# Second half of an expert gather: whole 8 KB rows instead of two 4 KB halves, and a new deal of the picks

## The reference

```python
qh = (t @ w_q).reshape(T, PEER_HEADS, 2, PEER_KEY_DIM // 2)
s = jnp.einsum('thpd,hpnd->thpn', qh, sub_keys)
s_top, i_top = lax.top_k(s, PEER_TOPK)                         # 16 of 128 keys, twice
cand = s_top[:, :, 0, :, None] + s_top[:, :, 1, None, :]
best, pos = lax.top_k(cand.reshape(T, PEER_HEADS, 256), PEER_TOPK)
idx = ...                                                      # 8 heads x 16 = 128 experts a token
g = jax.nn.softmax(best, axis=-1)
ue = jnp.take(u_tab, idx, axis=0)                              # rows of 1024 floats
ve = jnp.take(v_tab, idx, axis=0)
act = jax.nn.gelu(jnp.einsum('thkd,td->thk', ue, t))
out = jnp.einsum('thk,thkd->td', g * act, ve)
```

## Time and profile before

| | us |
|---|---|
| median of 3 runs | 3298.09 |
| lowest, highest | 3291.09, 3308.55 |
| the profiled execution | 3280.68 |
| its span | 3278.9 |
| PE busy | 2841.7 (87%) |
| DVE busy | 2060.0 (63%) |
| ACT busy | 1282.5 (39%) |
| gathers' queue, share of the DMA engines | 41.7% |
| granted TensorE clock, mean | 0.93 of full speed |

### The profile page before, as it was taken

The page is one execution under the profiler, slowest core; times in us unless marked ns, Lnnn a source line. Parts: engine busy times, 40 slices in busy tenths (PEclk is TensorE's granted clock), DMA queues, the critical chain, the costliest instruction groups (busy, mean ns, idle before and its releaser), DMA issues. The chain is left out here.

```text
span 3278.9 us, 41066 instructions
## 1 busy us (share of the span) xinstructions
PE 2841.7 (87%) x13812; PEld 2036.1 (62%) x13812; DVE 2060.0 (63%) x4500; ACT 1282.5 (39%) x2910; POOL 856.8 (26%) x773
## 2 busy tenths in 40 slices
PE   6999898887888887788899999787888997799998
PEld 6777777532344442455565666455777896678886
DVE  6785454478686775777644444754666878664445
ACT  3346423343334343546444222353544443442222
POOL 0000000243434345546656566651000000000000
PEclk9999799998999999889998999898898998799999
DMA  6531022699999999879989999985313453132221
GB/s 242 203 110 64 33 90 78 242 397 410 391 405 418 420 398 410 301 301 371 364 320 386 359 409 409 379 295 185 110 57 98 160 185 119 65 103 90 96 96 52
DMA packets 181883, 788.61 MB, mean 241 GB/s; under 512 B 19392, under 2 KB 22592, under 8 KB 148672
## 3 DMA queue, kind: packets, MB, share of 16 engines
q0 software_dynamic: 110592, 536.92, 41.7%
q1 hardware_dynamic: 65424, 229.90, 20.0%
q10 hardware_dynamic: 5680, 19.40, 1.7%
HBM read 784.05 MB, written 2.10 MB: 240 GB/s over the span
## 5 line engine op out<-in xcount | busy, mean ns | idle before, releaser
L2180 DVE SCALAR_TENSOR_TENSOR slots<-slots,work 128x1024 f32<-128x1024 f32 x508 | 621.9, 1224 | 202.5 <-DMA slots<-in_experts,consts 164.9
L895 PE MATMUL psum<-slots,acc 128*128 128x512 f32 x1008 | 492.4, 639 | 121.6 <-ACT acc L1487 115.1
L571 POOL DMA_INDIRECT slots<-in_experts,consts x252 | 286.2, 1136 | 987.2 <-DVE consts L2152 583.0
L895 PEld LDWEIGHTS psum<-slots,acc 128*128 128x128 f32 x1008 | 197.2, 202 | 398.1 <-issue 216.1
L1801 DVE TENSOR_TENSOR wlo<-w,whi 128x1024 fp32r<-128x1024 f32 x261 | 316.9, 1219 | 91.3 <-ACT whi L1283 90.5
L590 POOL DMA_INDIRECT slots<-in_expert_u,consts x256 | 286.7, 1120 | 286.5 <-DVE slots L2180 193.0
L1283 ACT ACTIVATE whi<-w 128x1024 fp32r<-128x1024 f32 x261 | 274.4, 1052 | 219.1 <-PE psum L641 212.0
L639 PE MATMUL psum<-xhi,whi 128*128 128x512 f32 x632 | 256.6, 406 | 1.9 <-DVE wlo L1801 1.9
L640 PE MATMUL psum<-xlo,whi 128*128 128x512 f32 x632 | 251.5, 398 | 0.0
L641 PE MATMUL psum<-xhi,wlo 128*128 128x512 f32 x632 | 251.4, 398 | 0.0
L626 PE MATMUL psum<-xres,w 128*128 128x256 f32 x1040 | 241.9, 387 | 0.0
(11 more groups left out here) (340 smaller groups left out, 5557.6 us busy)
## 6 DMA issues: line engine op xcount, KB each, us to landing
w<-in_stream SPq DMA_DIRECT2D x408, 512.0 KB
arena<-in_wmod SPq DMA_DIRECT2D x4, 2048.0 KB, 17.8
arena<-in_wmod ACTq DMA_DIRECT2D x8, 1024.0 KB, 6.7
acc<-in_wmod ACTq DMA_DIRECT2D x8, 1024.0 KB, 7.9
slots<-in_expert_u,consts POOLq DMA_INDIRECT x256, 8.7
slots<-in_experts,consts POOLq DMA_INDIRECT x252, 10.9
slots<-in_expert_v,consts POOLq DMA_INDIRECT x160, 9.0
xres<-in_xT SPq DMA_DIRECT2D x1, 2048.0 KB, 14.9
```

Source lines behind the costliest of these rows:

```text
L571: pool.indirect_dma_start(out=slots[slot], out_offset=None, in_=a["experts"], in_offset=bass.IndirectOffsetOnAxis(ap=indices[:, p:p + 1], ...
L895: mm = pe.matmul(bank(6 + half), diag(p), v[:, half * T:(half + 1) * T], start=(c == 0), stop=(c == PICKS - 1))
L2180: dve.scalar_tensor_tensor(u, u, 1.0, tokens[:, p // PICKS, :], ALU.mult, ALU.mult, accum_out=inner[:, c:c + 1]).then_inc(sem("dotted"), 1)
```

## The change

Three things change.

1. **Gather.** `gather_u` and `gather_v` are gone. All 512 picks use `gather`: one 8 KB row for each token into a slot, which is free when PE has used the pick. At pick 256 slot 7 is taken out of use (its place is `y_h` of the second block), which leaves eight; at pick 300 slot 9 joins, in the arena, once all 16 units are found. PE's own wait for v rows goes, since the row has landed before its dot.
2. **Deal.** The tiles' lengths are now 1.7 in lstm0, 2.4 in core0, 1.2 in lout0, 1.6 in xq0, 1.2 in xo0, 0.95 in mlp0, 2.0 in pool0, 1.7 in xq1 and 1.2 in xo1; the gap after mlp0 has 8 instead of 6.
3. **Search.** `LATE_UNITS` is 14 and units 1 to 13 stand at every 18th pick from 2 to 218; units 14 and 15 stand at 257 and 268. None stands at 279 or 290 any more.

What the planner's table gives, as the pick that the stage's last tile ends with, and the pairs that PE sums in each stage (the first tiles of a stage are multiplied together, and two picks of a gap follow them, so they count to the next stage):

| stage | tiles | picks end, before | after | pairs, before | after |
|---|---|---|---|---|---|
| lstm0 | 82-98 | 292 | 304 | 13 | 19 |
| core0 | 99-106 | 322 | 329 | 15 | 12.5 |
| lout0 (gap to 340, 347) | 107-114 | 335 | 342 | 8 | 8 |
| xq0 | 115-122 | 352 | 364 | 7 | 9.5 |
| xo0 (gap to 370, 381) | 123-130 | 365 | 376 | 8 | 7.5 |
| mlp0 | 131-194 | 469 | 461 | 50.5 | 41 |
| gap, pool0 (to 487, 481) | 195-196 | 482 | 477 | 8 | 9 |
| xq1 | 197-204 | 500 | 499 | 7.5 | 10 |
| xo1 | 205-212 | 512 | 512 | 6 | 6.5 |

```diff
-    core = range(SECTIONS["core0"][0], SECTIONS["lout0"][0])
-    gaps = {SECTIONS["lout0"][0] + 7: 3.5, SECTIONS["pool0"][0] + 1: 3.5, SECTIONS["mlp0"][0] + 63: 6,
+    weights = {"lstm0": 1.7, "core0": 2.4, "lout0": 1.2, "xq0": 1.6, "xo0": 1.2, "mlp0": 0.95, "pool0": 2.0, "xq1": 1.7,
+               "xo1": 1.2}
...
+    gaps = {SECTIONS["lout0"][0] + 7: 3.5, SECTIONS["pool0"][0] + 1: 3.5, SECTIONS["mlp0"][0] + 63: 8,
...
-SLOT_OPENS = {228: 6}
+SLOT_OPENS = {228: 6, 300: 9}
...
-    for p in range(EARLY):
+    for p in range(NPICKS):
+        if p == EARLY:
+            free.remove(7)
...
-LATE_UNITS = 12
-TOP_AT = {u: 2 + 21 * (u - 1) if u < LATE_UNITS else EARLY + 1 + 11 * (u - LATE_UNITS) for u in range(1, UNITS)}
+LATE_UNITS = 14
+TOP_AT = {u: 2 + 18 * (u - 1) if u < LATE_UNITS else EARLY + 1 + 11 * (u - LATE_UNITS) for u in range(1, UNITS)}
...
+                elif q is None and slot == 9:
+                    pool.wait_ge(sem("picked"), UNITS)
...
-            for p in range(EARLY):
+            for p in range(NPICKS):
                 gather(p)
-            for p in range(EARLY, NPICKS + LEAD):
-                if p < NPICKS:
-                    gather_u(p)
-                if p >= EARLY + LEAD:
-                    gather_v(p - LEAD)
...
-                for q in (p - 1, p):
-                    row, _, uses = V_USE[q - EARLY]
-                    pe.wait_ge(sem(f"v_in{row}"), 16 * uses)
                 pe.wait_ge(sem("diagonal"), p + 1)
...
-                                           v_row(q)[rows, half * T:(half + 1) * T], start=(c == 1),
+                                           slots[SLOT[q]][rows, D + half * T:D + (half + 1) * T], start=(c == 1),
...
-                if p < EARLY:
-                    dve.wait_ge(sem(f"experts_in{SLOT[p]}"), 16 * SLOT_USES[p])
-                    u = slots[SLOT[p]][:, 0:D]
-                else:
-                    row, _, uses = U_USE[p - EARLY]
-                    dve.wait_ge(sem(f"u_in{row}"), 16 * uses)
-                    u = u_row(p)
+                dve.wait_ge(sem(f"experts_in{SLOT[p]}"), 16 * SLOT_USES[p])
+                u = slots[SLOT[p]][:, 0:D]
```

## The result

| | before | after |
|---|---|---|
| median of 4 runs, us | 3300.98 | 3258.56 |
| lowest, highest | 3291.09, 3308.55 | 3252.68, 3266.46 |
| profiled execution, its span | 3280.68, 3278.9 | 3252.68, 3250.9 |
| ratio, 95% interval | | 0.9871 (0.9842 to 0.9900) |

One thing has to be known to read all that follows: the kernel before does not take the same time on every occasion (its medians on six occasions, on several chips, are 3278, 3301, 3303, 3305, 3326 and 3331 us), while kernels with whole rows took 3254 to 3268 us on all six. So a ratio is compared only with ratios of the same occasion.

The account below looks back on a forecast made before the run. PE and DMA were taken as overfull in mlp0 with room in lstm0, where DVE sets the pace. Terms (mlp0 -23, core0 -4.8, lstm0 -2.5, others mostly losses) summed to -15.7 us: 3282.4 us, range 3262 to 3316.

Parts of the forecast that it names:

- the 3% of bandwidth: Gathers at full DMA: 422 GB/s with 1 MB whole rows against 409 with halves; lstm0's second half would be 2 us shorter.
- a pair priced at 1.9 us: Every stage from lstm0 to xo1: each pair of picks moved in or out costs TensorE (PE) 1.9 us.

Follow-up runs that it names:

- before_third: The kernel before, unchanged, run and profiled again on a later occasion, beside the kernel before at 3331.2 us: 3332.4 us.

## What to carry to other kernels

Before a profile's stretch is priced, ask whether the execution is typical: three later profiles of this kernel had lstm0 and core0 at 231 to 251 us where the one read had 220, and in the two slowest that was 31 of the 49 and 55 us by which they were longer from lstm0 to the end of xo1. Here fewer and larger gathers were worth more than the 3% of bandwidth that they add; the still stretches of other engines go with POOL's long runs of gathers, but how much of the gain that is stays open. A new deal of work between stages pays only where a stage has an engine that really idles; a pair priced at 1.9 us cost 3.5 and more in the stages that took it in.

## What was not expected of the hardware

- A kernel whose second part gathers 4 KB rows took 3278 to 3331 us, by occasion, and on one chip 3326 and later 3303; with 8 KB rows it took 3254 to 3268 on the same occasions. The queue of the gathers goes from 110592 to 73728 packets, 144 for each gather of either size:

```profile
q0 software_dynamic: 110592, 536.92, 41.7%
```
```profile
q0 software_dynamic: 73728, 536.90, 41.2%
```

- In three of four profiles of the kernel before DVE and ACT stand up to 14.1 us with their input ready while POOL issues gathers without a gap. The still stretches are the same in two chips' profiles to some hundredths of a microsecond (10.96 and 10.94, 10.58 and 10.59, 4.23 and 4.20 us at line 2401). In these profiles many landings of gathers have no record either, and the page gives no time from issue to landing for the half rows, where it gave one before (8.7 and 9.0 us). The changed kernel's profile (after) lacks them too, so the missing records are a mark of the occasion and not of the half rows. What holds the signal back, and why on some occasions only, stays open. Of before_third's twelve still stretches eight overlap with no fetch of instructions at all, so these are not the cause.
- The rate at full DMA isn't what differs between the occasions. It is 409 GB/s in before_third too, as in the earlier trace rows:

```profile
1960.00:2130.00 170.00, 165.18 (x924) 110.69 (x923) 78.70 (x135) 48.53 (x171) 112.08 (x101) 1.00 1.03 409
```
